# Expert stage of a two-block network: the input-row turn and the middle-layer turn placed between the gate and the up product

## The reference, cut to what matters

```python
# 512 tokens of width 1024, 32 experts, each token goes to its 2 best experts
def expert_block(args):
    tok, wt, ex = args
    xb = hf[tok]                                # rows of the tokens of one expert
    a = xb @ w_gate[ex]                         # 1024 -> 512
    u = xb @ w_up[ex]                           # 1024 -> 512
    y = (jax.nn.silu(a) * u) @ w_down[ex]       # 512 -> 1024
    return y * wt[:, None].astype(y.dtype)
...
out = jnp.zeros((n, d), h.dtype).at[row_tok].add(ys.reshape(n_rows, d).astype(h.dtype))
```

## Time and profile before

| | us |
|---|---|
| median of three executions | 3950.08 |
| profiled execution, its own time | 3955.45 |
| span of the profiled execution | 3953.7 |
| expert stage on TensorE, first transposes to last down product | 3312.5 to 3925.9 |
| mean granted TensorE clock, share of full | 0.917 |

### The profile page before, as it was taken

The page is one execution under the profiler, slowest core; times in us unless marked ns, Lnnn a source line. Parts: engine busy times, 40 slices in busy tenths (PEclk is TensorE's granted clock), DMA queues, the critical chain, the costliest instruction groups (busy, mean ns, idle before and its releaser), DMA issues.

```text
span 3953.7 us, 39828 instructions
## 1 busy us (share of the span) xinstructions
PE 3454.4 (87%) x16724; PEld 2358.5 (60%) x16724; DVE 1106.1 (28%) x1759; ACT 1103.4 (28%) x1874; POOL 710.5 (18%) x344
## 2 busy tenths in 40 slices
PE   7987899979848988988879999988899986889896
PEld 5665578856537777756558877454686553333332
DVE  2633220132573333343331022246230121000001
ACT  3423342434432211212334342133321121111110
POOL 3121144422200000002114432000142121010001
PEclk9998899988878877879999999998999987999998
DMA  3321153321100000023112222210032235998996
GB/s 101 98 93 54 43 166 109 130 70 59 54 0 1 1 1 1 12 64 101 43 43 96 96 86 98 85 44 11 22 96 70 75 136 235 385 373 344 381 384 278
DMA packets 217760, 448.63 MB, mean 113 GB/s; under 512 B 14192, under 2 KB 191376, under 8 KB 204656
## 3 DMA queue, kind: packets, MB, share of 16 engines
q1 hardware_dynamic: 200832, 400.58, 27.8%
q10 hardware_dynamic: 6720, 25.17, 1.7%
q0 software_dynamic: 10032, 20.35, 1.5%
HBM read 502.67 MB, written 31.46 MB: 135 GB/s over the span
## 4 chain that ended last, share of the span: by engine, by line
PE 74%; DVE 11%; DMA 7%; ACT 4%; issue 3%; POOL 1%; SPq 0%; ACTq 0%; POOLq 0%; DVEq 0%
PE product_banks L526 12%; PE product_banks L528 12%; PE product_banks L527 12%; PE product_banks L505 7%; PE product_banks L1692 5%; DMA A<-in_w_up 3%; PE product_banks L1725 3%; DMA Wr<-expert_rows 3%; PE product_banks L561 2%; PE product_banks L2139 2%; PE stat_bank L599 2%; PE product_banks L2129 1%; PE product_banks L2131 1%; PE product_banks L965 1%; PE product_banks L1172 1%
## 5 line engine op out<-in xcount | busy, mean ns | idle before, releaser
L443 POOL TENSOR_TENSOR Wr_parts<-Wr,Wr_parts 128x1024 fp32r<-128x1024 f32 x266 | 639.4, 2405 | 1989.1 <-ACT Wr_parts L423 1989.1
L527 PE MATMUL product_banks<-A_parts,Wr_parts 128*128 128x512 f32 x2128 | 846.2, 398 | 0.0
L423 ACT ACTIVATE Wr_parts<-Wr 128x1024 fp32r<-128x1024 f32 x266 | 280.9, 1059 | 1043.9 <-PE product_banks L528 986.2
L526 PE MATMUL product_banks<-H_parts,Wr_parts 128*128 128x512 f32 x1168 | 478.7, 410 | 62.2 <-DVE A_parts L455 37.7
L527 PEld LDWEIGHTS product_banks<-A_parts,Wr_parts 128*128 128x128 f32 x2128 | 408.9, 192 | 99.7 <-issue 11.4
L528 PE MATMUL product_banks<-H_parts,Wr_parts 128*128 128x512 f32 x1168 | 468.2, 401 | 0.0
L526 PE MATMUL product_banks<-A_parts,Wr_parts 128*128 128x512 f32 x960 | 397.2, 414 | 46.9 <-POOL Wr_parts L443 31.3
L528 PE MATMUL product_banks<-A_parts,Wr_parts 128*128 128x512 f32 x960 | 378.8, 395 | 0.0
L1692 PE MATMUL product_banks<-A,Wr 128*64 128x512 f32 x1504 | 340.4, 600 | 19.4 <-DMA A<-in_w_up 17.1
L526 PEld LDWEIGHTS product_banks<-H_parts,Wr_parts 128*128 128x128 f32 x1168 | 224.1, 192 | 134.8 <-issue 42.1
L1692 PEld LDWEIGHTS product_banks<-A,Wr 128*64 128x64 f32 x1504 | 113.3, 139 | 241.7 <-issue 238.7
(11 more groups left out here) (392 smaller groups left out, 4147.6 us busy)
## 6 DMA issues: line engine op xcount, KB each, us to landing
A<-in_w_gate SPq DMA_DIRECT2D x32, 2048.0 KB
A<-in_w_up SPq DMA_DIRECT2D x32, 2048.0 KB
A<-in_w_down SPq DMA_DIRECT2D x32, 2048.0 KB
Wr<-in_m_w_up SPq DMA_DIRECT2D x32, 1024.0 KB, 5.3
Wr<-in_m_w_down SPq DMA_DIRECT2D x32, 1024.0 KB, 4.8
Wr<-in_w_in SPq DMA_DIRECT2D x32, 1024.0 KB, 5.7
Wr<-in_c_w_kv SPq DMA_DIRECT2D x16, 1024.0 KB, 5.1
expert_rows<-LB ACTq DMA_DIRECT2D x12, 1024.0 KB, 4.6
```

The source lines that it names most:

```text
L423: nc.scalar.activation(weight_parts(s)[0], loaded_part(s), ACT.Copy).then_inc(*mark("weights_high", s))
L443: nc.gpsimd.tensor_tensor(lo, loaded_part(s), hi, ALU.subtract).then_inc(*mark("weights_split", s))
L526: pe.matmul(bank[:, :], hi[:, k, :], x_hi, start=(kk == 0), stop=False)
L527: pe.matmul(bank[:, :], hi[:, k, :], x_lo, start=False, stop=False)
```

## The change

The middle turn becomes functions of its own on both engines, and cycle b on TensorE becomes: gate(b), turn of the middle layer of b-1, turn of the input rows of b+1, up(b), down(b-1). The order on ScalarE follows. No instruction is added or removed, and no wait is dropped.

```diff
         def experts_pe(pe):
+            last = len(PAIRS) - 1
             pair_turn_pe(pe, 0)
-            pair_up_pe(pe, 0)
-            pair_turn_pe(pe, 1)
-            for b in range(1, len(PAIRS)):
+            for b in range(len(PAIRS)):
+                pair_gate_pe(pe, b)
+                if b:
+                    hidden_turn_pe(pe, b - 1)
+                if b < last:
+                    pair_turn_pe(pe, b + 1)
                 pair_up_pe(pe, b)
-                if b + 1 < len(PAIRS):
-                    pair_turn_pe(pe, b + 1)
-                pair_down_pe(pe, b - 1)
-            pair_down_pe(pe, len(PAIRS) - 1)
+                if b:
+                    pair_down_pe(pe, b - 1)
+            hidden_turn_pe(pe, last)
+            pair_down_pe(pe, last)
...
         def experts_act(act):
+            last = len(PAIRS) - 1
             pair_rows_act(act, 0)
-            pair_silu_act(act, 0)
-            pair_rows_act(act, 1)
-            for b in range(1, len(PAIRS)):
+            for b in range(len(PAIRS)):
                 pair_silu_act(act, b)
-                if b + 1 < len(PAIRS):
+                if b:
+                    hidden_turn_act(act, b - 1)
+                if b < last:
                     pair_rows_act(act, b + 1)
-                pair_out_act(act, b - 1)
-            pair_out_act(act, len(PAIRS) - 1)
+                if b:
+                    pair_out_act(act, b - 1)
+            hidden_turn_act(act, last)
+            pair_out_act(act, last)
```

More of the change, by code:

```diff
@@ L1696, in pair_product_pe, with pair_gate_pe @@
             mm.then_inc(*mark("unit_used", (kind, b)))
-        def pair_up_pe(pe, b):
+        def pair_gate_pe(pe, b):
             pe.wait_ge(*at("pair_rows_ready", (b, 1)))
@@ L1704, in pair_up_pe @@
             pair_product_pe(pe, "gate", b)
+        def pair_up_pe(pe, b):
             if b:
@@ L1707, in pair_up_pe, with hidden_turn_pe @@
             pair_product_pe(pe, "up", b)
-        def pair_down_pe(pe, b):
+        def hidden_turn_pe(pe, b):
             pe.wait_ge(*at("hidden_ready", b))
@@ L1715, in pair_down_pe @@
             mm.then_inc(*mark("hidden_turned", b))
+        def pair_down_pe(pe, b):
             pe.wait_ge(*at("hidden_turned_ready", b))
@@ L1755, in pair_silu_act, with hidden_turn_act @@
                 *mark("silu_ready", b))
-        def pair_out_act(act, b):
+        def hidden_turn_act(act, b):
             act.wait_ge(*at("hidden_turned", b))
@@ L1762, in pair_out_act @@
                 *mark("hidden_turned_ready", b))
+        def pair_out_act(act, b):
             act.wait_ge(*at("unit_used", ("down", b)))
```

## The result

The changed kernel takes 3994.21 us (median of four, 3991.39 to 4007.92) against 3949.95 us before: the ratio is 1.0113, with a 95% interval of 1.0082 to 1.0143. I had said 3997. The same kernel, measured again later beside other runs, gave 3994.13 us, ratio 1.0115 (1.0093 to 1.0136).

The account below looks back on a forecast made before the run. Transfers were taken to pace each three pairs until the extra pair's rows land, then TensorE. Seven periods at +5.2, +0.5 at the start, -2.6 at the end and +12.7 clock gave +47.0 on 3950.1: 3997 us, 8-in-10 range 3979 to 4013.

Parts of the forecast that it names:

- The ScalarE waits go and a cycle without waits takes 22.3 us: TensorE's 24 waits of 1.18 us for the middle-layer copy vanish; a cycle falls from 23.58 us, 1.3 us less.
- Three kinds of cycle, waits of 9.3, 4.7 and 0 us: TensorE's row waits: 9.3 us ahead of an extra pair, 4.7 in the extra pair's cycle, none in the next.
- 100 us instead of 44.0: Sign of being right: TensorE's total row-turn waits for expert rows in the new profile, some 15 times.
- The landing stays at T + 66.1: Next extra pair's rows land 66.1 us after T, the start of an extra pair's cycle, ending a full transfer line.
- line starves: Rival: late up product delays asking for pair 8's second up load, 2 us per period; +20, 4017 us; chance 13%.
- the clock behind the waits of 4.7 us: Clock loss after the extra pair cycle's row wait lies ahead of the landing, beside full transfers: 0.
- my sum without the clock: Three-pair period grows 5.2 us from 75.84; with start and end, +34.3 us in all before clock loss.
- Landing to the next T is 14.97 plus 2.2 of clock: Behind the extra rows' landing stand row turn, start, up and down, 14.97 us instead of 9.74, plus half-clock loss.
- The clock, 15.4 us: TensorE resumes at half clock behind the 9.3 us waits, losing 2.2 us at each of 7 places.
- Start and end: Fourth pair's rows land slightly later, +0.5 us; two full cycles behind the last such landing gain 2.6 us.
- The sum, +47.0: Whole kernel's slowdown: 34.3 us without the clock plus 12.7 us net clock, giving 3997 us.

Follow-up runs that it names:

- both kinds of waits filled: Changed kernel plus unread identity transposes ahead of the row turn, 68 before an extra pair and 28 in the extra pair's own cycle: 3988.7 us, ratio 1.0089.
- filling the long waits: Changed kernel plus 68 unread identity transposes ahead of the row turn in the 7 cycles before an extra pair: 3988.1 and 3977.1 us.
- the early asking: Kernel before, with SP asking for input rows one cycle sooner, ahead of the previous pair's up weights: 3914.94 us, ratio 0.9940.

## Why the prediction was right, step by step

- *The ScalarE waits go and a cycle without waits takes 22.3 us*: 22.32 us. The start of a product right behind transposes, which the trace before did not show, costs about 0.1 us (3538.55 to 3539.09 for four transposes, 0.54, against 0.45 between the two groups before).
- *Three kinds of cycle, waits of 9.3, 4.7 and 0 us*: 8.5, 4.0 and 0. TensorE comes to the wait 7.7 us behind the cycle's start, not 7.4 (3502.63 to 3514.35, less 4.01), and the rows take 11.1 instead of 11.5 us. Neither matters to the sum, which goes by the landing. The "100 us instead of 44.0" of the signs set waits without the one at the start against waits with it; like for like it is 117 instead of 44, or 89 instead of 16.
- *The landing stays at T + 66.1*: over six periods 66.6 to 68.0, mean 67.2, where the same six before have 65.8 to 67.2, mean 66.3. The line of transfers grew by 0.9 us. This fits the "line starves" rival in small: the up product of the extra pair's cycle ends later, at half clock, and with it the asking for the second up load. It is also where the prediction put a term at nothing, the clock behind the waits of 4.7 us, that is not nothing: with both kinds of waits filled that product ends 19.0 to 19.9 us behind T instead of 21.1 to 22.7, and the landing is back at T + 66.0 in the mean. The distance from landing to landing is there 80.6 and 82.2 us in two periods, mean over five 81.2, against the 81.1 of my sum without the clock.
- *Landing to the next T is 14.97 plus 2.2 of clock*: 16.81 and 17.79 in the rows above, mean of seven 17.2, in the second profile 16.7; 14.9 where the wait is filled. Before it is 10.2 in the mean of seven and not 9.74, since the clock falls behind some of the short waits there.
- *The clock, 15.4 us*: 15.6 by filling the long waits. That the two agree so well is in part luck, since 3 us of the second do not lie where the first was placed.
- *Start and end*: taken +0.5 and -2.6; the first extra pair's rows land 90.0 us behind the stage's start instead of 88.4.
- *The sum, +47.0*: +44 in the medians, +40 in those of the second measurement, +50 and +53 in the stages of two profiles. The 53 are made up of +1.6 at the start, +5.2 in the line (six times), +48.6 from the landings to the next T (seven times) and -2.0 at the end; the prediction has in the same places +0.5, 0, +49.3 and -2.6. The terms that were too small are the line's and the start's. So the mechanism was right and its stage short by 3 to 6 us; that the medians came within 3 us of the forecast is better than the account deserves.

What I had not seen is how much the rows' lateness cost before the change already: I priced the early asking at 20 us in the kernel before, and it gave 23 in the stage, 24 by the ratio and 34 in the medians of its chip.

## What to carry to other kernels

Before a consumer is moved forward in an engine's order, look up when the thing that it waits for was asked for and what stands ahead of it in its queue; a wait that is short or absent today may be the end of a line of transfers that does not move. What was hidden beside that line and now stands behind it is the price, not the wait itself. Here the cure was one line in the list of transfers, and after it the place of the row turn made no difference.

## What the runs showed of the hardware that I had not expected

- Where the clock stood at half behind a wait of 8 to 9 us, 7.6 us of transposes that nobody reads in the wait kept it at full in seven places of seven in both profiles of that kernel, and were worth 1.8 to 2.3 us a place between the rows' landing and the next extra pair's cycle. In the kernel with both kinds of waits filled it still fell in two places of seven.
- Identical code ahead of the stage took 3290.6 to 3315.7 us in fourteen profiles. In two of them, of one and the same kernel, the granted clock between 1500 and 2000 us of the span was 0.85 (stage from 3311.5) and 0.88 (from 3293.7). What sets this was not tried.
- The row load of an extra pair took 14.6 to 16.3 us behind weights on SP's queue and 10.5 to 11.7 us on ScalarE's, beside DMA engines as full (share 0.88 from 3470.22 to the landing in the changed kernel; 0.94 over the cycle 3535.76 to 3563.70 in the other).
